# A hybrid decoder layer on one core: POOL's gate and scaling in the scan moved, the scan's small products spread over the passes, low parts given to VectorE

## The reference

```python
h = rmsnorm(x, norm_mix_w)
proj = h @ w_in                                 # columns: z | xbc | dt | q | k | v | f
xbc = silu(causal_dwconv(xbc))                  # xs (16 heads x 64), Bm, Cm (2 groups x 128)
dt  = softplus(dt + dt_bias);  a = dt * A;  cum = cumsum(a) in each chunk of 128 tokens
# for each of 4 chunks (l, s: tokens of the chunk; g: group; r: head of the group)
CB     = Cm . Bm                                          # 128 x 128 a group
y_diag = (CB * exp(cum_l - cum_s) [causal] * dt_s) @ xs
states = Bm^T @ (xs * dt * exp(cum_end - cum_s))
h_in   = exp(cum_end) * h_in(previous) + states(previous)
y_off  = (Cm @ h_in) * exp(cum_l)
y      = y_diag + y_off + xs * d_skip
y_ssm  = rmsnorm(y * silu(z))
y_att  = rmsnorm(forgetting_attention(rmsnorm(q), rmsnorm(k), v, log_f))
x = x + concat(y_ssm, y_att) @ w_out
x = x + mixture_of_experts(rmsnorm(x))          # 32 experts, two a token, 96 MB of weights
```

## Time and profile before

| | |
|---|---|
| median of 3 runs | 722.3 us (721.61 to 722.89) |
| the profiled execution | 722.08 us, span 720.3 us |
| TensorE busy | 677.6 us, 94% of the span |
| VectorE, ScalarE, POOL busy | 389.8, 291.2 and 149.0 us |
| HBM | 157.67 MB read, 20.28 MB written |
| mean granted TensorE clock | 0.981 of 2.4 GHz |

### The profile page before, as it was taken

How to read it: one execution, slowest core, us unless ns; L and a number is a source line. 1 busy time by engine, 2 the same in 40 slices (tenths; PEclk the granted TensorE clock), 3 DMA queues, 4 the chain that set the end, 5 groups by cost and what they waited for, 6 DMA issues and landing times.

```text
span 720.3 us, 10643 instructions
## 1 busy us (share of the span) xinstructions
PE 677.6 (94%) x3850; PEld 468.5 (65%) x3850; DVE 389.8 (54%) x834; ACT 291.2 (40%) x651; POOL 149.0 (21%) x178
## 2 busy tenths in 40 slices
PE   8999999999999999999999999979999978888975
PEld 7878888777777888766767788867434323333442
DVE  6866678878879665777787554471222211122211
ACT  5934534465655545665666423221212111121200
POOL 2300010114222110022342232020132321122331
PEclk9999999999999999999999999989999999999998
DMA  8333255426264343191030079689999999999993
GB/s 297 94 115 117 79 174 162 132 74 173 80 158 146 88 147 102 46 361 49 16 103 1 1 287 421 242 350 369 412 416 417 403 410 398 425 417 413 413 402 129
DMA packets 61160, 162.77 MB, mean 226 GB/s; under 512 B 14185, under 2 KB 25605, under 8 KB 49841
## 3 DMA queue, kind: packets, MB, share of 16 engines
q1 hardware_dynamic: 49120, 144.64, 53.7%
q0 software_dynamic: 6880, 9.02, 4.2%
q10 hardware_dynamic: 5104, 8.39, 3.1%
HBM read 157.67 MB, written 20.28 MB: 247 GB/s over the span
## 4 chain that ended last, share of the span: by engine, by line
PE 25%; SPq 14%; DMA 5%; DVE 2%; issue 2%; ACT 2%; POOL 0%; POOLq 0%; DVEq 0%; ACTq 0%
SPq L427 6%; PE bank L1816 5%; DMA s_gu<-in_w_expert_gate_dram 4%; SPq L475 4%; SPq L461 4%; PE bank L1845 3%; PE bank L1405 3%; PE bank L1407 3%; PE bank L1406 3%; PE bank L1787 2%; PE bank L1681 1%; PE bank L1638 1%; PE bank L1621 1%; PE bank L1763 1%; PE bank L1610 1%
## 5 line engine op out<-in xcount | busy, mean ns | idle before, releaser
L1816 PE MATMUL bank<-s_gu,s_xgT 128*64 128x512 f32 x352 | 84.4, 635 | 16.3 <-DMA s_gu<-in_w_expert_up_dram 16.3
L282 DVE TENSOR_TENSOR s_wl<-s_raw,s_wh 128x512 fp32r<-128x512 f32 x105 | 89.9, 903 | 12.3 <-ACT s_wh L1022 12.1
L1022 ACT ACTIVATE s_wh<-s_raw 128x512 fp32r<-128x512 f32 x120 | 72.7, 628 | 42.1 <-PE bank L1407 18.6
L1405 PE MATMUL bank<-s_wh,s_hTh 128*128 128x512 f32 x192 | 78.7, 410 | 0.0
L1407 PE MATMUL bank<-s_wh,s_hTl 128*128 128x512 f32 x192 | 75.1, 391 | 0.0
L1816 PEld LDWEIGHTS bank<-s_gu,s_xgT 128*64 128x64 f32 x352 | 28.8, 146 | 71.0 <-issue 71.0
L1406 PE MATMUL bank<-s_wl,s_hTh 128*128 128x512 f32 x192 | 74.9, 390 | 0.0
L1321 ACT ACTIVATE s_sg<-bank,s_slot_scale 128x256 f32<-128x256 f32 x16 | 7.6, 473 | 151.6 <-PE bank L1816 113.2
L1845 PE MATMUL bank<-s_dn,s_hidT 128*64 128x512 f32 x256 | 58.5, 598 | 1.6 <-DVE s_hidT L2388 1.6
L2388 DVE COPY s_hidT<-bank 128x256 f32<-128x256 f32 x16 | 6.8, 423 | 93.7 <-PE bank L1825 93.7
L2421 DVE SCALAR_TENSOR_TENSOR s_yrow<-bank,s_slot_scale,s_xg 128x512 f32<-128x512 f32 x30 | 21.2, 746 | 46.1 <-PE bank L1845 46.1
(11 more groups left out here) (307 smaller groups left out, 1392.9 us busy)
## 6 DMA issues: line engine op xcount, KB each, us to landing
s_dn<-in_w_expert_down_dram SPq DMA_DIRECT2D x28, 1024.0 KB, 26.9
s_gu<-in_w_expert_gate_dram SPq DMA_DIRECT2D x26, 1024.0 KB, 28.0
s_gu<-in_w_expert_up_dram SPq DMA_DIRECT2D x24, 1024.0 KB, 28.0
s_raw<-in_w_in_dram SPq DMA_DIRECT2D x88, 256.0 KB, 4.1
s_raw<-in_w_out_dram SPq DMA_DIRECT2D x32, 256.0 KB, 3.5
s_gu<-in_w_expert_up_dram SPq DMA_DIRECT2D x12, 512.0 KB, 9.4
s_decay_rows<-decay_rows SPq DMA_DIRECT2D x4, 1024.0 KB, 4.7
s_gu<-in_w_expert_gate_dram SPq DMA_DIRECT2D x8, 512.0 KB, 8.8
```

The costliest lines, as they stand in the source:

```text
L282: eng.tensor_tensor(low, full, high.bitcast(F32), ALU.subtract).then_inc(sem(f"{what}_low_{low_engine(what, i)}"), 1)
L1022: act.activation(wh[:, i % HL, :], raw[:, i % RAW, :], ACT.Copy).then_inc(sem("w_high"), 1)
L1405: pe.matmul(dst, ah, bh, start=start, stop=False)
L1816: last = pe.matmul(ps[j][r, :].rearrange("p (w f) -> p w f", w=2), m["xgT"][:, j, k, r], gu[:, half, :, k, :], start=(k == 0), stop=(k == ...
```

## The change

It touches the scan and the low parts:
- POOL's `gate(c)` waits for the same additions as before and, for c < 3, for both states of the chunk as well (`state_kept`). `scaled_x(c)` waits for the chunk's last masked product (`m_done`), and in the loop it stands behind `skip_term` instead of ahead of it.
- VectorE no longer copies `y` onto itself in chunk 0 (that only counted `y_whole`); who waited for it waits for `y_diag`, and the counts of `y_whole` are one chunk lower.
- TensorE: `cb(0)` two tiles later; `diag(c, 0)` and `diag(c, 1)` one tile later in the chunk's third pass; `diag(c, 2)` and `diag(c, 3)` no longer behind that pass but in the chunk's fourth pass, behind its second and fourth tile.
- ScalarE takes the first square ahead of the table load, and the exponentials of `dte` and `etot` behind the first decays; VectorE's product that needs them is moved behind `m_product(0, 1)`.
- VectorE makes the low parts of slots 98 to 118 with an even number, eleven in all, that POOL made.

```diff
-LOW_BY_DVE, LOW_BY_BOTH = (6, *range(HL, 11 * 8 + HL)), 11 * 8 + HL
+LOW_BY_DVE = (6, *range(HL, 15 * 8))
...
             def load_decay_out(c):
 
-                sp.wait_ge(sem("y_whole"), 2 * c)
+                if c == 1:
+                    sp.wait_ge(sem("y_diag"), 2)
+                else:
+                    sp.wait_ge(sem("y_whole"), 2 * (c - 1))
...
             def load_first_bias():
-                sp.wait_ge(sem("y_whole"), 2 * TC)
+                sp.wait_ge(sem("y_whole"), 2 * (TC - 1))
...
             def scaled_x(c):
 
                 if c < TC - 1:
+                    pool.wait_ge(sem("m_done"), 4 * c + 4)
                     if c:
                         pool.wait_ge(sem("state_done"), 2 * c)
...
             def gate(c):
 
-                pool.wait_ge(sem("y_whole"), 2 * c + 2)
+                if c:
+                    pool.wait_ge(sem("y_whole"), 2 * c)
+                else:
+                    pool.wait_ge(sem("y_diag"), 2)
+                if c < TC - 1:
+                    pool.wait_ge(sem("state_kept"), 2 * c + 2)
                 pool.wait_ge(sem("z_stored"), TC + c + 1)
...
             for c in range(TC - 1):
                 causal_decays(c + 1)
                 gate(c)
+                skip_term(c + 1)
                 scaled_x(c + 1)
-                skip_term(c + 1)
...
-                    for i in slot_after(n, k):
-                        if low_engine("w", i) == "pool":
-                            weight_low(pool, i)
                     if n == N_AO - 1 and k == 0:
                         sum_squares(NHP - 1)
-            lows(KC * 13 + HL, NSLOT)
+            pool.wait_ge(sem("ay_summed"), NHP)
...
+            qk_square(0)
             act.preload_act_table_set("natural_log_exp_and_others")
-            act.wait_ge(sem("steps_known"), 4)
-            act.activation(dte[:], dte[:], ACT.Exp).then_inc(sem("dt_acts"), 1)
-            act.activation(etot[:], tot[:, :, 0:H], ACT.Exp).then_inc(sem("dt_acts"), 1)
             for i in range(16):
                 n = N_QK + i
-                qk_square(i)
+                if i:
+                    qk_square(i)
...
                     if i:
                         decay_out_exp(i // 4)
+                    else:
+                        act.wait_ge(sem("steps_known"), 4)
+                        act.activation(dte[:], dte[:], ACT.Exp).then_inc(sem("dt_acts"), 1)
+                        act.activation(etot[:], tot[:, :, 0:H], ACT.Exp).then_inc(sem("dt_acts"), 1)
...
-                    if i == 1 and k == 1:
+                    if i == 1 and k == 3:
                         cb(0)
-                    if i >= 2 and i % 4 == 2 and k in (1, 3):
-                        diag(i // 4, k // 2)
+                    if i >= 2 and i % 4 == 2 and k in (2, 4):
+                        diag(i // 4, k // 2 - 1)
+                    if i >= 2 and i % 4 == 3 and k in (1, 3):
+                        diag(i // 4, 2 + k // 2)
...
                 if step == 1:
                     if c:
                         y_off(c, 1)
-                    diag(c, 2)
-                    diag(c, 3)
...
-                else:
-                    dve.tensor_copy(y[:, cols], y[:, cols]).then_inc(sem("y_whole"), 1)
```

More of the change, by code:

```diff
@@ L2122, in _ @@
                 qk_scale(i)
[L2123 to L2126, removed]
                 c = i // 4
@@ L2130, in _ @@
                     m_product(c, 1)
+                    if c == 0:
+                        dve.wait_ge(sem("dt_acts"), 5)
+                        dve.tensor_tensor(dte[:], dte[:], sp[:, :, 0:H], ALU.mult).then_inc(sem("scales_known"), 1)
+                        dve.wait_ge(sem("scales_known"), 1)
                 if i % 4 == 1:
```

## The result

| | before | after |
|---|---|---|
| median of the timed runs | 722.3 us (721.6 to 723.4) | 737.1 us (734.7 to 739.0) |
| the profiled execution | 722.08 us | 738.36 us |

A forecast was written before the change was run, and what follows sets the result against it. The prediction took dense TensorE work to bound the kernel up to 565 us, then SyncE's expert weight loads. Its terms summed to +14.2 us on the 722.3 us median, giving 736.5 us, range 727 to 745.

The forecast's parts named there:

- head of chunk 0: Start of the scan: with less VectorE work, chunk 0's states are kept at about 170.1 instead of 174.5: -4.4 us.
- kept state to y_off, three chunks: Scan, chunks 1 to 3: this stretch grows to 17.5 us through the late gate: +3.25, +3.4 and +2.8 us.
- y_off to kept state, without clock: Scan, chunks 1 and 2: later masked products and low parts lengthen this stretch to 18.4 us: +1.2 and +2.5 us.
- behind chunk 3, without clock: End of the scan: the last transpose of k waits for the later low parts: +1.7 us.
- clock: TensorE in the scan: granted clock falls behind two long idle stretches, 1.6 us each: +3.2 us.
- low parts: Attention's fourth pass: four low parts moved to VectorE cost slightly more than POOL's absence wins: +0.5 us.
- The late gate and who stands behind it: Scan: the gate delays SyncE's loads of `y`, then `decay_out` (6.3 us), so kept state to exponential takes 9.3 us.
- The step from the exponential to y_off: Scan: 1.05 us of exponential, then 7.15 us to y_off, taken from chunk 2 of the earlier trace.
- The mild rival: Scan chain binds mildly: `decay_out` at its lower bound, no clock loss, attention unchanged; 730 us, down to 727; chance 0.25.
- Spreading: TensorE's masked products in the scan: eight groups standing alone cost 1.6 us and delay low parts and kept states.
- The first rival (hidden gate): Scan: `decay_out` lands in time, the late gate stays hidden and the change is faster, 721 or 720 us; chance 0.09.
- the harsh one: Scan chain binds with an 8.0 us load, third clock loss and attention at 1.8 us: +22.2, 745 us; chance 0.12.

The follow-up runs named there:

- kernel 5: Kernel before the change with only the eleven even low parts of slots 98 to 118 given to VectorE; 722.0 us.
- kernel 3: Changed kernel with the load of `decay_out` issued ahead of `y`'s in SyncE's queue, the gate still late; 721.6 us.
- kernel 4: Changed kernel without the gate's wait for `state_kept` and with TensorE's masked products back at their old places; 717.5 us.
- kernel 1: Changed kernel without the gate's wait for `state_kept`, all else of the change kept; 724.0 us.
- kernel 12: Changed kernel with both loads still behind the late gate, but `decay_out` issued ahead of `y`; 727.7 us.
- kernel 7: Changed kernel with 24 identity products filling TensorE's wait ahead of the second y_off of chunks 2 and 3; 733.4 us.
- kernel 2: Kernel before the change with only the gate's wait for `state_kept` added; 729.5 us.
- kernel 10: Kernel before the change with only TensorE's masked products spread as in the change; 729.1 us.
- kernel 6: Changed kernel, gate still late, with TensorE's masked products back at their old places; 728.5 us.
- kernel 11: Changed kernel without the gate's `state_kept` wait, masked products at old places, low parts of slots 98 to 118 on POOL; 717.6 us.

## Why the prediction was right

The mechanism was right. That the total came out within 0.6 us is in part luck: one term was 4.5 us too small and another 3 us too large, and they cancelled. Against the earlier trace rows, to the last transpose of the profiled execution:

| step | predicted | measured |
|---|---|---|
| head of chunk 0 | -4.4 | 170.06 - 174.50 = -4.4 |
| kept state to y_off, three chunks | +9.45 | 18.80, 18.57, 19.59: +4.55 + 4.47 + 4.88 = +13.9 |
| y_off to kept state, without clock | +3.7 | 16.96 and 18.36 - 1.56: -0.25 + 0.93 = +0.7 |
| behind chunk 3, without clock | +1.7 | 17.47 - 1.72 - 13.54 = +2.2 |
| clock | +3.2 | +3.3 |
| low parts | +0.5 | none measurable (kernel 5) |
| sum | +14.2 | +15.6 to the last transpose, +16.3 in the whole execution |

The 0.7 us behind the last transpose no experiment places; from there to the end it is 457.5 to 459.7 us in the profiled executions of the change, the kernel before and kernels 3 and 4. The profiled execution of the change is 1.3 us above its median; the medians differ by 14.8.

*The late gate and who stands behind it* was right as a mechanism (kernels 1, 3) and too small as a term: the 6.3 us for `y` and then `decay_out` were 7.4, 7.3 and 8.3 from `y`'s issue to the exponential, nearer to the upper bound of 8.0 than to my figure and once above it. I had reasoned that an empty queue ahead makes the landing quick. `y` did land quicker (median 4.9 us against 6.5 in the earlier trace rows), but what counts is the half megabyte of `y` ahead of `decay_out`, and kernel 12 shows it. The step from the exponential to y_off (1.05 + 7.15) was right: 8.3, 8.2, 8.2.

*y_off to kept state* is off by 3 us the other way. The start of the low parts was right (7.2 us behind y_off; 7.4 in chunk 1, 7.3 in chunk 2 of kernel 7). But I took 6.50 us for the seven in chunks 1 and 2, a row in which POOL worked beside them, though the change had just moved that work away; they took 4.9 and 4.7. The mild rival had this figure (seven times 0.68), but was added up wrongly: three stretches at 4.8 instead of 6.5 take 5.2 us from 730, which is 725 and not 727. Kernel 2 shows the relief by itself: 14.11 us from y_off to kept state with 4.8 us of low parts. With two, one and no POOL operation beside the seven they take 8.16, 6.45 and 4.8 us (kernels 10, 1 and 2). In kernel 1 a single low part bears it, which ends 0.5 us behind the gate (193.35 to 196.07), where the others take 0.7:

```profile
193.78 2.83 DVE L282 TENSOR_TENSOR s_wl<-s_raw,s_wh 128x512 fp32r<-128x512 f32 x1
```

By the Trainium skill ("SBUF — State Buffer", the part on who interferes with whom) a VectorE instruction with two inputs in SBUF and a GpSimd one that reads SBUF block each other for the whole instruction; this row agrees, and I had used it for the gate's new place but not for the place it left.

*Spreading* was priced as one term of 5.4 us against the kernel before. Its own price is 6.4 (early gate) to 8.6 us (late). TensorE's part was somewhat small: 0.6 us in each of two loops, so 2.4 if four chunks cost the same, against 1.6 in all. The rest is that low parts and kept state come later.

*The head*: the figure is right by accident. I had the low parts start 0.9 us earlier and take 3.5 us less; they start 0.15 us later (161.44 against 161.29) and take 4.6 us less (5.4 against 9.99). The late start belongs to this execution: ScalarE waited 2.9 us until 102.69 for a store of conv rows issued at 94.03, ahead of all that was changed, and the first transpose stood at 148.38, where it was at 147.26 to 147.59 in kernels 3, 7 and 12, whose chunk 0 is that of the change. These keep the first state at 168.7 to 169.1, so the head is worth 5.4 to 5.8 us.

*The clock* was right in place and size (+3.3 us, kernel 7), in the profiled execution; its windows now show the fall to 0.50 in the scan, which no row did before. The first rival (hidden gate) is refuted: it asked for `decay_out` within 2.9 us behind the gate; it took over 7. The mild rival had the load too early, the harsh one a third fall of the clock.

## What to carry to other kernels

Before an instruction is made to wait, list the in-order queues behind its semaphore, DMA queues first: here one wait on an engine with an 18% share held back a load that it had no business with, and the order of two DMA issues was worth 15.5 us. A duration is to be taken from a row whose company is that of the changed kernel: a low part costs 0.6 us alone, and 1.2 to 1.4 on average where two or three POOL operations ran beside seven of them (8.16 us in kernel 10, 9.99 in the earlier trace rows). Two edits that lengthen the same loop are not priced one by one: alone on the kernel before the late gate costs 7.2 us and spreading 6.9, and with the -4.6 of kernel 11 that would make 9.5, where the change costs 14.8. And a part of a change can be good (head, dropped copies and POOL's order, -4.6 us together) while the whole is 2% slower.

## What was not expected of the hardware

Waits of TensorE of 2.0 to 2.5 us between dense work sometimes cost clock and sometimes not: none was lost behind 2.38 us (the change, chunk 1), 2.18 (kernel 2, chunk 1), 2.12 and 2.47 (kernel 12), while the granted clock fell to 0.50 for one window of 2 us and to 0.67 to 0.73 for another behind 2.39 and 2.23 us (kernel 2, chunks 2 and 3) and 2.27 us (kernel 6, chunk 2), and to 0.52 and 0.63 behind 1.97 us (kernel 6, chunk 3). In these rows the length alone doesn't decide it; what does stays open. It may be a part of why runs of kernel 2 spread from 726.4 to 731.3 us (mean granted clock 0.979 and 0.976 in the two fastest, 0.973 to 0.976 in the others), which was not tested.
